# How expert slots get their token rows: scattering rows against scattering token numbers, in a two-layer diffusion step with top-2-of-8 experts

## The reference, cut to what matters

```python
logits = einsum('nd,de->ne', xf, router)             # 640 x 8
probs = softmax(logits); top_p, top_i = top_k(probs, 2)
top_p = top_p / sum(top_p)
gates = sum(one_hot(top_i, 8) * top_p[..., None], axis=1)
for e in range(8):                                   # expert width 1408, all float32
    y = y + gates[:, e:e+1] * ((silu(xf @ w_gate[e]) * (xf @ w_up[e])) @ w_down[e])
```

## Time and profile before

| | |
|---|---|
| median of 3 runs | 2141.05 us |
| the profiled execution's own time | 2143.72 us |
| its span, first to last instruction | 2141.8 us |
| TensorE busy | 2058.5 us (96%) |
| mean DMA rate | 213 GB/s; about 386 GB/s in the expert loop |
| mean granted TensorE clock | 0.993 of full speed |

### The profile page before, as it was taken

One profiled execution on the slowest core, in us unless ns is written; L12 is line 12 of the kernel. 1 busy time (PEld: TensorE's weight loads), 2 busy tenths in 40 slices (PEclk: granted clock), 3 DMA queues, 4 the chain that ended last, 5 costly groups with the idle time before them and its releaser, 6 DMA issues. The chain is left out here.

```text
span 2141.8 us, 31732 instructions
## 1 busy us (share of the span) xinstructions
PE 2058.5 (96%) x12186; PEld 1791.4 (84%) x12186; DVE 1361.1 (64%) x1433; ACT 1147.5 (54%) x1412; POOL 150.0 (7%) x161
## 2 busy tenths in 40 slices
PE   5999999999999999999989998999999999999997
PEld 3898667999999999989856887888888888888884
DVE  5436643544433444653853367998998889989997
ACT  3316653422211222442754346778777777787874
POOL 0030000000000000012000025100000000000003
PEclk8999999999999999999999999999999999999998
DMA  9220045246422212322004329999999999999995
GB/s 314 88 86 6 1 158 186 90 148 235 144 74 79 79 54 73 118 81 68 6 34 173 129 89 392 386 387 388 387 386 386 386 386 386 386 388 386 386 387 190
DMA packets 282078, 455.58 MB, mean 213 GB/s; under 512 B 13200, under 2 KB 160768, under 8 KB 281984
## 3 DMA queue, kind: packets, MB, share of 16 engines
q1 hardware_dynamic: 269216, 419.92, 55.4%
q0 software_dynamic: 8576, 30.97, 3.8%
q10 hardware_dynamic: 4192, 3.34, 0.5%
HBM read 426.77 MB, written 27.44 MB: 212 GB/s over the span
## 5 line engine op out<-in xcount | busy, mean ns | idle before, releaser
L1842 DVE TENSOR_TENSOR w_lo<-mraw,w_hi 128x1792 fp32r<-128x1792 f32 (+2 forms) x306 | 643.5, 2114 | 90.6 <-ACT w_hi L1200 89.0
L1200 ACT ACTIVATE w_hi<-mraw 128x1792 fp32r<-128x1792 f32 (+2 forms) x306 | 541.8, 1775 | 175.1 <-PE ps L2532 153.1
L2530 PE MATMUL ps<-w_hi,xs_lo 128*128 128x448 f32 (+1 forms) x816 | 310.6, 381 | 7.9 <-DVE w_lo L1842 6.6
L2532 PE MATMUL ps<-w_hi,xs_hi 128*128 128x448 f32 (+1 forms) x816 | 305.6, 375 | 0.0
L2531 PE MATMUL ps<-w_lo,xs_hi 128*128 128x448 f32 (+1 forms) x816 | 305.1, 374 | 0.0
L1321 DVE TENSOR_TENSOR sub_lo<-zone,sub_hi 128x1024 fp32r<-128x1024 f32 (+2 forms) x113 | 130.8, 1159 | 229.5 <-ACT sub_hi L881 229.5
L2530 PEld LDWEIGHTS ps<-w_hi,xs_lo 128*128 128x128 f32 x816 | 153.5, 188 | 34.2 <-DVE w_lo L1842 15.1
L2532 PEld LDWEIGHTS ps<-w_hi,xs_hi 128*128 128x128 f32 x816 | 153.5, 188 | 19.2
L2531 PEld LDWEIGHTS ps<-w_lo,xs_hi 128*128 128x128 f32 x816 | 153.7, 188 | 17.8
L1559 DVE TENSOR_REDUCE stat<-ps 128x2 f32<-128x1536 f32 (+3 forms) x80 | 92.4, 1157 | 119.7 <-PE ps L2212 98.9
L881 ACT ACTIVATE sub_hi<-zone 128x1024 fp32r<-128x1024 f32 (+2 forms) x113 | 110.1, 976 | 106.9 <-PE ps L2097 93.7
(11 more groups left out here) (346 smaller groups left out, 3497.2 us busy)
## 6 DMA issues: line engine op xcount, KB each, us to landing
mraw<-in_moe_w_down SPq DMA_DIRECT2D x68, 1024.0 KB, 14.0
mraw<-in_moe_w_gate SPq DMA_DIRECT2D x68, 896.0 KB, 13.1
mraw<-in_moe_w_up SPq DMA_DIRECT2D x68, 896.0 KB, 14.2
zone<-in_w_ada SPq DMA_DIRECT2D x48, 1024.0 KB, 5.9
mraw<-in_moe_w_gate SPq DMA_DIRECT2D x34, 1024.0 KB, 15.6
mraw<-in_moe_w_up SPq DMA_DIRECT2D x34, 1024.0 KB
mraw<-in_moe_w_down SPq DMA_DIRECT2D x34, 768.0 KB, 13.4
zone<-in_w_in SPq DMA_DIRECT2D x14, 1024.0 KB, 5.2
```

Source lines behind the costliest of these rows:

```text
L1200: nc.scalar.activation(w_hi[:, n % SPLITS, a], mraw[:, n % MRING, a], ACT.Copy).then_inc(w_hi_ready, 1)
L1842: nc.vector.tensor_tensor(w_lo[:, n % SPLITS, a], mraw[:, n % MRING, a], w_hi[:, n % SPLITS, a].bitcast(f32), ALU.subtract).then_inc(w_spl ...
L2530: nc.tensor.matmul(out, a_lo, b_hi, start=start, stop=False)
L2532: return nc.tensor.matmul(out, a_hi, b_hi, start=False, stop=stop)
```

## The change

The scatter of rows is replaced by a scatter of numbers. The five tiles of `htok` are stored once, in token order, to the DRAM tensor `token_rows`; SyncE issues these five stores between pieces 4 and 5. GpSimd scatters 4-byte token numbers to `slot_tokens`, a DRAM tensor with one number per slot row, by ten indirect DMAs of 128 numbers. For every slot it loads the slot's 128 numbers to `token_of`, one per partition, and gathers the 128 rows of `token_rows` that they name to `xs` by an indirect DMA. Padding rows have the number 0 and therefore carry token 0's row, which nobody reads afterwards. The clearing of `xperm`, its waits and the zeroed tile are gone; in their place two small DMAs by GpSimd in layer 0 load the numbers 0 to 639 and clear `slot_tokens`. Pieces 6 to 8 wait for the five stores instead of the scatters. In GpSimd's loop the load of the next rows stands behind the landing of the store to `yslots`.

```diff
-XTILES = SLOTS + 2
-    xperm = nc.dram_tensor("xperm", (XTILES * P, D_MODEL), f32).ap()
+    token_rows = nc.dram_tensor("token_rows", (T, D_MODEL), f32).ap()
+    slot_tokens = nc.dram_tensor("slot_tokens", (SLOTS * P, 1), i32).ap()
+        token_i, token_of = sb("token_i", [P, TT], i32), sb("token_of", [P, 1], i32)
...
                 piece(n)
-                z = n - PIECE_AT[("up", 0)] - 1
-                if z == 0:
-                    sp.wait_ge(zeroed, 1)
-                if 0 <= z < XTILES:
-                    for h in range(2):
-                        sp.dma_start(xperm[z * P:(z + 1) * P, 512 * h:512 * h + 512], zeros[:]).then_inc(zero_rows, 16)
...
                 if n == 5:
-                    sp.wait_ge(htok_ready, TT)
+                    for t in range(TT):
+                        sp.wait_ge(htok_ready, t + 1)
+                        sp.dma_start(token_rows[t * P:(t + 1) * P, :], htok[:, t, :]).then_inc(rows_out, 16)
                 if n == 6:
                     sp.wait_ge(first_x, 1)
-                if n >= 6:
-                    sp.wait_ge(scattered[n - 6], 16 * SCATTERS[n - 6])
+                    sp.wait_ge(rows_out, 16 * TT)
                 expert_piece(e0, n)
...
                 if l == 0:
-                    pool.wait_ge(main_done, MAIN[("o", 0, KC - 1)] + 1)
-                    nc.gpsimd.memset(zeros, 0.0).then_inc(zeroed, 1)
+                    pool.dma_start(token_i[:], d["token_i"]).then_inc(no_tokens, 16)
+                    pool.dma_start(slot_tokens, d["no_tokens"]).then_inc(no_tokens, 16)
...
             pool.wait_ge(rows_ready, 1)
-            pool.wait_ge(zero_rows, 16 * 2 * XTILES)
+            pool.wait_ge(no_tokens, 32)
             for t in range(TT):
-                pool.wait_ge(htok_ready, t + 1)
                 for c in range(2):
                     pool.indirect_dma_start(
-                        out=xperm, out_offset=bass.IndirectOffsetOnAxis(ap=rowi[:, c, t:t + 1], axis=0),
-                        in_=htok[:, t, :], in_offset=None).then_inc(scatter_of(t), 16)
-            for n in range(3):
-                pool.wait_ge(scattered[n], 16 * SCATTERS[n])
-            pool.dma_start(xs, xperm[P:2 * P, :]).then_inc(xs_in, 16)
+                        out=slot_tokens, out_offset=bass.IndirectOffsetOnAxis(ap=rowi[:, c, t:t + 1], axis=0),
+                        in_=token_i[:, t:t + 1], in_offset=None).then_inc(tokens_out, 16)
+            pool.wait_ge(tokens_out, 16 * 2 * TT)
+
+            def slot_tokens_in(at):
+                pool.dma_start(token_of[:], slot_tokens[at, :]).then_inc(tokens_in, 16)
+
+            def slot_x():
+                pool.indirect_dma_start(out=xs, out_offset=None, in_=token_rows,
+                                        in_offset=bass.IndirectOffsetOnAxis(ap=token_of[:, 0:1], axis=0)).then_inc(xs_in, 16)
+
+            slot_tokens_in(slice(P, 2 * P))
+            pool.wait_ge(tokens_in, 16)
+            pool.wait_ge(rows_out, 16 * TT)
+            slot_x()
             pool.drain().then_inc(y_left, 1)
...
             with pool.Fori(0, SLOTS - 2) as s:
-                pool.wait_ge(etr_done, 2 + G_ETR + 5 * s + TR_OF["xb"] + 1)
-                pool.dma_start(xs, xperm[bass.ds((s + 2) * P, P), :]).then_inc(xs_in, 16)
+                pool.wait_ge(xs_in, 16 * (s + 1))
+                slot_tokens_in(bass.ds((s + 2) * P, P))
                 pool.wait_ge(y_evac, s + 2)
                 pool.dma_start(yslots[bass.ds(s * P, P), :], ybuf).then_inc(y_stored, 16)
+                pool.wait_ge(etr_done, 2 + G_ETR + 5 * s + TR_OF["xb"] + 1)
+                pool.wait_ge(tokens_in, 16 * (s + 2))
                 pool.wait_ge(y_stored, 16 * (s + 1))
                 pool.sem_inc(y_left, 1)
+                slot_x()
...
-                    act.wait_ge(zero_rows, 16 * 2 * XTILES)
                     modulate(1, 1, 0, ks=range(3))
```

More of the change, by code:

```diff
@@ L440, in build @@
         spare = arena[:, h_split_at + (HJ - KC) * T:h_split_at + KC * TX]
-        token_scale, up_part, zeros = spare[:, 0:T], spare[:, T:2 * T], spare[:, 2 * T:2 * T + D_MODEL // 2]
+        token_scale, up_part = spare[:, 0:T], spare[:, T:2 * T]
         late_rows_t = arena[:, ATT + 1024 + RING * RING_F:ATT + 2048 + RING * RING_F].rearrange("p (u n) -> p u n", u=2)
@@ L512, in build @@
         w_used, cond_zero = sem("w_used"), sem("cond_zero")
-        ones_ready, zeroed, zero_rows = sem("ones_ready"), sem("zeroed"), sem("zero_rows")
+        ones_ready = sem("ones_ready")
         layer_w_in, cache_k_in, cache_v_in, cache_c_in = ([sem(f"{n}{l}") for l in range(DEPTH)] for n in
@@ L540, in build @@
         htok_scaled, htok_ready = sem("htok_scaled"), sem("htok_ready")
-        scattered = [sem(f"scattered{n}") for n in range(3)]
+        no_tokens, tokens_out, tokens_in, rows_out = (sem(n) for n in ("no_tokens", "tokens_out", "tokens_in", "rows_out"))
         shift_row_ready, xg_ready, router_ready = sem("shift_row_ready"), sem("xg_ready"), sem("router_ready")
@@ L573, in pieces_done @@
             return SPLITS + NPC * s + n + 1
-        def scatter_of(t):
-            return scattered[t // 2]
-        SCATTERS = (4, 4, 2)
         N_LAYER_W = 4
@@ L2643, in constants @@
     group = np.tile(np.eye(32), (4, 1))
+    out["token_i"] = np.arange(T, dtype=np.int32).reshape(TT, P).T
+    out["no_tokens"] = np.zeros((SLOTS * P, 1), np.int32)
     out["small"] = np.concatenate([np.broadcast_to(small, (P, small.size)), group, np.tile(swap(p), (4, 1))], axis=1).astype(np.float32)
```

## The result

The changed kernel takes 2150.16 us (median of 20 runs, 2145.03 to 2159.89), the kernel before 2141.56 us beside it (20 runs, 2139.08 to 2145.09). The ratio is 1.0042, its 95% interval 1.0036 to 1.0049. The kernel became 8.6 us slower where 5.6 us of gain were forecast, and the time lies above the range given.

What follows compares the result with a forecast made beforehand. TensorE and DMA were taken as matched in the loop, whose start waits for the first nine pieces. Sums of 4.7 (6.15 - 1.3 - 0.2 + 0.06) and 6.6 us gave 5.6 us gain: 2135.4 us, range 2132 to 2143.

Steps and rivals of the forecast that it cites:

- Token numbers: Before the loop: ten scatters' 1280 four-byte packets at 16 ns cost 1.3 us over 16 engines; bounds 0 and 5.9.
- nearest row: Profile row for the 4-byte store to gate_rows, used to price a small packet at 16 ns of engine time.
- The clearing: Between 410 and 561 us: removing 38 clearing stores of 256 KB gains 0, at most 2 us.
- Ten scatters become five stores: Ahead of piece 6: half the bytes gain 6.15 us of queue; two sums gave 4.7 and 6.6 us overall.
- The new wait: Piece 6 waits for all five stores to land, leaving a queue gap of 0.2 us, bounds 0 to 3.
- an empty queue before piece 6: Sign named beforehand as showing the forecast wrong: DMA engines run empty before piece 6's load.
- GpSimd's program and the loop: GpSimd's number landings, fetches and gathers, about 6.5 us a landing, stay hidden before and in the loop; 0.
- 47.9 that the prediction named as wrong: Expert loop: slot period should stay 47.8 us; a period over 47.9 would show the forecast wrong.
- Matched sides: Expert loop: TensorE needs 47.8 us a slot, DMA 47.4 at 387 GB/s, leaving DMA 0.4 us spare.
- Numbers cost several times 16 ns: Case within the rival of a gap behind the stores: dearer number packets leave 1 to 4 us gain; rival's chance 0.14.
- gap rival: Behind the stores: late landing, empty engines or dearer numbers leave about 2.5 us gain, 2138.6 us; chance 0.14.
- Slower: padding: Loop gathers: padding rows all reading token 0's row hold the engines, 5 to 6 us net loss, 2147 us; chance 0.08.

Runs made afterwards that it cites:

- e1: Changed kernel without the ten scatters of token numbers, slot_tokens loaded from a constant (75 mixed numbers, 53 zeros per slot); 2137.21 us, 0.9981 of the kernel before.
- e6: Changed kernel with each token number scattered as a 64-byte row, side by side; 2140.29 us, 0.9986 of the kernel before.
- e8: Kernel before with every clearing store issued twice, the second to another tensor; 2141.33 us, 0.9998 of the kernel before.
- e14: Changed kernel with 4-byte numbers, 16 neighbours per 64-byte block but blocks 4 KB apart; 2156.32 us, 1.0063 of the kernel before.
- e5: Changed kernel with 4-byte numbers written 512 bytes apart; 2141.83 us, 1.0000 of the kernel before.
- e15: Changed kernel with 4-byte numbers written 32 bytes apart, two to a block of 64; 2140.45 us, 0.9993 of the kernel before.
- e4: Changed kernel with each token number scattered as a 512-byte row; 2142.34 us, 1.0006 of the kernel before.
- e11: e9 with all slots' numbers fetched once ahead of the loop, and GpSimd's loop written out with gather and store only; 2139.72 us, 0.9987 of the kernel before.
- e13: Changed kernel with 4-byte numbers in the same 8.7 KB but neighbouring rows 68 bytes apart; 2139.53 us, 0.9985 of the kernel before.
- e12: e1 with all token numbers 0, so nearly every slot reads only token 0's row; 2142.30 us, 0.9992 of the kernel before.
- e7: e4 with the five stores issued ahead of piece 3 instead of piece 5; 2139.37 us, 0.9997 of the kernel before.
- e9: e6 with the five stores issued ahead of piece 3 instead of piece 5 (both repairs); 2137.77 us, 0.9974 of the kernel before.
- e2: Changed kernel without the five stores, gathers reading a constant tensor, number scatters kept; 2138.95 us, 0.9992 of the kernel before.
- e3: Changed kernel with the ten number scatters issued only after the five stores have landed; 2158.06 us, 1.0077 of the kernel before.
- e10: Changed kernel with 4-byte numbers written 64 bytes apart; 2141.07 us, 0.9994 of the kernel before.

## Why the prediction was wrong

**The step that failed** is "Token numbers", the term of 1.3 us with the bounds 0 and 5.9. Measured it is 13.0 us (after less e1), or 9.9 us against the same numbers as 64-byte rows (e6; 12.0 by the two ratios). Its unit was the time that a packet holds one engine. By that view the prediction even took too much: the numbers' queue shows 320 packets, not the 1280 of the prediction, and 1.0% of 29 us, which is 0.3 us. But the cost isn't in their own packets. Where the numbers of a scatter meet in one small block, the packets of the other queue, with the weights and stores, are slow. The "nearest row", the store to gate_rows, could not show this. It is an ordinary store of two transfers, not ten scatters in flight together. Its targets too lie 4 bytes apart, but most of its packets ran when the weights beside them were through (from 1200 to 1206 the engines moved 28 GB/s), so there was little to hold up. It priced a packet, and I took that for the whole cost. The upper bound shared the same assumption, so it was no bound. The page DMA: Bandwidth & Descriptors of the Trainium skill (Specifications) says that a transfer below 512 bytes is read, modified and written. I put that down as priced by rows 9. Here the size is not what decides: 4 bytes at a distance of 32 to 512 bytes cost little or nothing, and the same 4 bytes side by side cost 10 us and more. That read-modify-write in one block is what makes the writers wait for each other would fit, but no run looks into it.

**The clearing, 0.** Right (e8).

**Ten scatters become five stores, 6.15 us.** Right within what can be told: without the jam piece 8 comes 4 to 6 us earlier (39.75 before; 33.6 to 35.8 in e1 and, without e8 and e14, in all from e5 to e15; 2.8 in e4, which writes 0.66 MB more), where 4.7 and 6.6 were forecast. With both repairs it is 5.9 us, and the time moves by 4.8.

**The new wait, 0.2 us (0 to 3).** Undersized, but within its bounds. In the changed kernel itself it is covered by the jam: the queue is not empty before piece 6 (358 GB/s at a share of 1.00 from 1301 to 1303). Without the jam the hole behind the stores is 1.6 to 2.0 us, and in e6 the stop of TensorE before piece 8 brings an estimated 1.7 us of a lower clock with it, which the sum had no term for. There the forecast sign "an empty queue before piece 6" appears, as 237 GB/s at a share of 0.72.

**GpSimd's program and the loop.** The landings were near 6.5 us as taken: fetch 4.7, gather 8.1, store 6.8 us in the median over the loop, and neither TensorE nor the queue of weights waits for them. TensorE is busy 291.98 of 292 us as before. But the period is 47.94 instead of 47.83, 1.5 us in all, beyond the 47.9 that the prediction named as wrong. Its cause is open, and so is whether the change makes it: kernels with the same work in the loop lie between 47.84 and 48.01, one execution each, and TensorE is busy 291.97 to 291.99 of 292 us in all of them. Nothing points at the fetch (e11), the gather (e13, e14) or the reading of one row (e12).

**Matched sides, 0.4 us of spare.** Not so. In the kernel after SyncE waits 142.1 us for buffers in 1400 to 1600, where it had waited 12.8, and while the queue was catching up the engines moved 406 GB/s. 18.35 MB at 406 GB/s are 45.2 us, a spare of 2.6 us a slot. The 387 of the kernel before was what TensorE's pace asks for (18.35 MB in 47.83 us are 384), with a queue that stood full.

**The rivals.** "Numbers cost several times 16 ns" named the right part, inside the gap rival, which still left a gain of 1 to 4 us. "Slower: padding" had the sign of the result and the wrong mechanism (e12). A rival in which the numbers slow the other queue was missing. The range was too narrow at its upper end for that reason: the chance of slower, 0.07, rested on padding and on unnamed losses beside it.

## What to carry to other kernels

A small write is not priced by its own packets. Ask who else writes to the same block of DRAM at that time: ten scatters in flight together, with targets 4 bytes apart, held up 6 MB of other traffic and cost 10 to 13 us, and giving every target 64 bytes of its own made that go, for 139 KB of DRAM (32 bytes did nearly as well). And a store whose landing gates a load should be issued with enough loads queued behind it to cover the landing: here three pieces closed the hole in the queue that one had left, though the gain in time isn't clear of the noise.

## What the runs showed of the hardware

- Share and rate of the DMA engines part company in a jam: 0.93 at 110 GB/s (after), 0.97 at 120 (e14). Share alone would have read as a full queue. The culprit's own queue shows 1.0%; the victim's shows 93.3%.
- 4-byte writes to DRAM by ten overlapping scatters: landing after the last issue 12.75 us side by side, 5.87 us at 512 bytes apart, 6.50 us at 64; 4 KB rows had taken 11.95.
- Sixteen neighbours in 64 bytes jam even with 4 KB between the blocks (e14), and the same numbers in 8.7 KB hardly do when consecutive rows are 68 bytes apart (e13: 289 to 330 GB/s at full share in two stretches of 5 us, against 79 to 226 for most of 1280 to 1300 in the kernel after).
- The loop's queue has two ways to run at the same TensorE load: full, with SyncE waiting 13 to 31 us in 200 at a share of 1.05 (before, e4, e6, e7, e8, e9, e11, e13, e14), or drained, with 142 to 150 us of waiting at 1.02 to 1.03 (after, e1, e2, e3, e5, e10, e12, e15). What decides between them is open. The slot period doesn't follow it.
